# Attention weights times values: one product of 512 columns in fp32 becomes three passes of 256 columns, and moves in the order of a block

## The reference, cut to what matters

```
scores = einsum("bqhrd,bshrd->bhrqs", qi, k) * scale - slopes * dist
probs  = softmax(scores, axis=-1)
w      = probs[:, :, 0] - lam * probs[:, :, 1]
o      = einsum("bhqs,bshe->bqhe", w, v)        # the product that is changed
o      = rms_norm(o, subln_g) * (1 - lam_init)
y_attn = o * silu(g)
```

## Time and profile before

| | us |
|---|---|
| median of 3 runs (lowest to highest) | 3786.94 (3786.23 to 3787.26) |
| the profiled execution, its own time | 3784.53 |
| its span, first to last instruction | 3782.8 |
| PE busy / DVE busy / ACT busy, share of the span | 95% / 60% / 44% |
| attention stage, first transposes to last | 1652 to 2284 |
| mean granted clock of PE | 0.98 |

### The profile page before, as it was taken

The page is one execution under the profiler, slowest core; times in us unless marked ns, Lnnn a source line. Parts: engine busy times, 40 slices in busy tenths (PEclk is TensorE's granted clock), DMA queues, the critical chain, the costliest instruction groups (busy, mean ns, idle before and its releaser), DMA issues.

```text
span 3782.8 us, 48362 instructions
## 1 busy us (share of the span) xinstructions
PE 3609.8 (95%) x20222; PEld 3036.7 (80%) x20222; DVE 2251.6 (60%) x2947; ACT 1668.6 (44%) x2123; POOL 468.9 (12%) x373
## 2 busy tenths in 40 slices
PE   8999989999998999999999989999999999999998
PEld 7778968888876787877777759978777888778998
DVE  4545353456666765655656662468889888843332
ACT  4333344431114544467667772145455554442132
POOL 0001032200000121200000000012222222210001
PEclk9999999999999899999999999999999999999999
DMA  3012023342212011011111123121111111153111
GB/s 110 23 40 90 26 81 109 112 159 89 89 69 90 23 34 40 18 51 34 37 28 34 29 86 140 42 82 34 45 45 39 56 51 45 34 213 110 45 40 67
DMA packets 227389, 244.85 MB, mean 65 GB/s; under 512 B 10007, under 2 KB 190180, under 8 KB 227172
## 3 DMA queue, kind: packets, MB, share of 16 engines
q1 hardware_dynamic: 222391, 224.92, 18.4%
q10 hardware_dynamic: 4781, 16.84, 1.2%
HBM read 191.40 MB, written 50.33 MB: 64 GB/s over the span
## 4 chain that ended last, share of the span: by engine, by line
PE 77%; DVE 12%; ACT 5%; issue 3%; DMA 1%; POOL 0%; SPq 0%; ACTq 0%; DVEq 0%; POOLq 0%
PE pd L211 63%; PE pq L211 11%; PE pd L366 2%; DVE t L3520 2%; DVE t L328 1%; DVE t L3528 1%; PE pq L366 1%; DVE t L3965 1%; ACT t L3125 1%; ACT t L320 1%; DVE t L3952 0%; DVE t L3950 0%; DVE t L3197 0%; DVE t L2078 0%; DVE t L3215 0%
## 5 line engine op out<-in xcount | busy, mean ns | idle before, releaser
L211 PE MATMUL pd<-t 128*128 128x512 f32 (+2 forms) x15104 | 2904.1, 353 | 32.5 <-ACT t L3716 9.8
L211 PEld LDWEIGHTS pd<-t 128*128 128x128 f32 x15104 | 2407.6, 191 | 459.8 <-issue 90.9
L211 PE MATMUL pq<-t 128*128 128x128 f32 (+5 forms) x3782 | 635.7, 330 | 75.0 <-DVE t L4001 15.7
L211 PEld LDWEIGHTS pq<-t 128*128 128x128 f32 (+2 forms) x3782 | 484.3, 181 | 187.4 <-issue 44.4
L320 ACT ACTIVATE t<-t 128x2048 fp32r<-128x2048 f32 (+3 forms) x133 | 212.6, 1599 | 633.2 <-PE pd L211 590.8
L328 DVE TENSOR_TENSOR t<-t 128x2048 fp32r<-128x2048 f32 (+3 forms) x133 | 257.3, 1935 | 173.7 <-ACT t L320 173.2
L1919 DVE TENSOR_TENSOR t<-pd,t 128x512 f32<-128x512 f32 x256 | 172.9, 689 | 104.9 <-PE pd L211 102.7
L3248 DVE COPY t<-pd 128x512 f32<-128x512 f32 x64 | 44.2, 691 | 218.6 <-PE pd L366 218.6
L3528 DVE SCALAR_TENSOR_TENSOR t<-t 128x1024 f32<-128x1024 f32 x120 | 173.8, 1448 | 0.5
L3520 DVE SCALAR_TENSOR_TENSOR t<-t 128x1024 f32<-128x1024 f32 x120 | 169.1, 1409 | 2.1
L3917 POOL TENSOR_TENSOR t<-t 128x512 f32<-128x512 f32 x56 | 96.0, 1714 | 592.8 <-ACT t L3861 299.4
(11 more groups left out here) (345 smaller groups left out, 2830.8 us busy)
## 6 DMA issues: line engine op xcount, KB each, us to landing
t<-in_w_in_dram SPq DMA_DIRECT2D x97, 512.0 KB, 4.3
t<-in_w_out_dram SPq DMA_DIRECT2D x20, 1024.0 KB, 5.4
t<-in_w_in_dram SPq DMA_DIRECT2D x16, 1024.0 KB, 5.3
t<-in_w_mlp_dram SPq DMA_DIRECT2D x64, 256.0 KB, 3.5
u_scratch<-t SPq DMA_DIRECT2D x64, 256.0 KB, 3.3
t<-in_w_mlp_dram SPq DMA_DIRECT2D x16, 1024.0 KB, 5.0
t<-u_scratch SPq DMA_DIRECT2D x15, 1024.0 KB, 7.2
t<-in_x_dram SPq DMA_DIRECT2D x16, 512.0 KB, 9.2
```

Of the source, the lines that this page charges most:

```text
L211: ins = e.matmul(out, l, r, start=(first and j == 0), stop=(last and j == n - 1), skip_group_check=True)
```

## The change

The product AV is formed per two blocks (256 columns) and not per four, in split parts: 24 matmuls of 128x256 for each quarter of a head in place of 8 fp32 matmuls of 128x512 for each half. For that:

- `WT` becomes two tiles of [128, 8, 256], high and low part, so it holds two blocks. ACT copies both groups of transposes as high parts (`wTh`), and DVE then subtracts to get the low parts (`wTc`). Both groups' banks are freed by DVE's `wTc`.
- The values are split likewise: ACT's copy gives the high part (`avh`), DVE's new `dve_att_vt` the low part (`avt`), and this frees the bank of vt.
- PE's order in block n becomes: [tt in 6, 7: vt]; [tt in 2, 5: ms]; projection of the next head; [tt even, n > 0: AV of the two blocks before]; scores(n+2); wT(n,0), wT(n,1).
- ACT reads each quarter of AV right behind the exponentials of n+2 (square and copy of 256 columns), ahead of its copies of wT(n). The order of the other steps of ACT and DVE stays.
- The ring `tmp` has 6 tiles in place of 4, and two waits name the last quarter of AV.

```diff
@@ -2857,10 +2857,16 @@
     QS = [[w[:, 1024:2048] for w in WH], [sbt(ph, [128, S], F32R) for _ in range(2)]]
     KS = [[w[:, 1024:2048] for w in WL[0:2]], [sbt(ph, [128, S], F32R) for _ in range(2)]]
     KL = [[WL[2][:, 1024:2048], sbt(ph, [128, S], F32R)], [sbt(ph, [128, S], F32R) for _ in range(2)]]
-    AB = [[sbt(ph, [128, S]), sbt(ph, [128, NT, 128])] for _ in range(2)]
+    AB = []
+    for _ in range(2):
+        raw = ExitStack()
+        gT32 = sbt(raw, [128, S])
+        v32 = sbt(raw, [128, NT, 128])
+        raw.close()
+        AB.append([sbt(ph, [128, S]), sbt(ph, [128, NT, 128], F32R), sbt(ph, [128, NT, 128], F32R), v32])
     SR = ring(ph, 3, [128, 2, S])
-    WT = sbt(ph, [128, 8, 512])
-    tmp = ring(ph, 4, [128, 512])
+    WT = [sbt(ph, [128, 8, 256], F32R) for _ in range(2)]
+    tmp = ring(ph, 6, [128, 512])
     sm = ring(ph, 4, [128, 8])
     epsc = sbt(ph, [128, 1])
     ph.close()
@@ -2918,7 +2924,7 @@
                 pe_att_fm(e, 0, kind, th)
 
     def act_att_out(e, h, kind, th):
-        gT, vt_ = AB[h % 2]
+        gT = AB[h % 2][0]
         sl, b = half(th), PD.of("a" + kind, h, th)
         e.wait_ge(*at["a" + kind, h, th])
         if kind in "qk" and h >= 2:
@@ -2950,9 +2956,17 @@
     def act_att_vt(e, h, th):
         e.wait_ge(*at["avT", h, th])
         if h >= 2:
-            e.wait_ge(*at["AV", h - 2, 1])
+            e.wait_ge(*at["AV", h - 2, 3])
         e.copy(AB[h % 2][1][:, th * 4:th * 4 + 4, :], four(PD.of("avT", h, th)[:, :])).then_inc(
-            *at.inc("act", "avt", h, th, free=("avT", h, th)))
+            *at.inc("act", "avh", h, th))
+
+    def dve_att_vt(e, h, th):
+        sl = slice(th * 4, th * 4 + 4)
+        e.wait_ge(*at["avh", h, th])
+        if h >= 2:
+            e.wait_ge(*at["AV", h - 2, 3])
+        e.tensor_tensor(AB[h % 2][2][:, sl, :], four(PD.of("avT", h, th)[:, :]), AB[h % 2][1][:, sl, :].bitcast(F32),
+                        SUB).then_inc(*at.inc("dve", "avt", h, th, free=("avT", h, th)))
 
     def dve_att_out(e, h, kind, th):
         sl, b = half(th), PD.of("a" + kind, h, th)
@@ -3011,14 +3025,16 @@
 
     def pe_att_values(e, n, bank):
 
-        h, th = n // 8, n // 4 % 2
-        b = at_bank(e, bank, "AV", h, th)
-        for m in range(n, n + 4):
+        h, q = n // 8, n // 2 % 4
+        b = at_bank(e, bank, "AV", h, q)
+        for m in range(n, n + 2):
             for q2 in range(2):
                 e.wait_ge(*at["wTc", m, q2])
         e.wait_ge(*at["avt", h, 0])
         e.wait_ge(*at["avt", h, 1])
-        mms(e, b[:, :], [(AB[h % 2][1][:, j, :], WT[:, j, :]) for j in range(8)]).then_inc(*at.inc("pe", "AV", h, th))
+        _, vh, vl, _ = AB[h % 2]
+        mms(e, b[:, 0:256], [p for j in range(8) for p in three(vh[:, j, :], vl[:, j, :], WT[0][:, j, :],
+                                                                WT[1][:, j, :])]).then_inc(*at.inc("pe", "AV", h, q))
 
     def pe_stage_att(e):
         for th in range(2):
@@ -3036,10 +3052,6 @@
         turns = cycle((2, 3))
         for n in range(BLOCKS):
             h, tt = divmod(n, NT)
-            if n + 2 < BLOCKS:
-                pe_att_scores(e, n + 2)
-            if tt % 4 == 0 and n:
-                pe_att_values(e, n - 4, next(turns))
             if tt >= 6 and h < 7:
                 pe_att_vt(e, h + 1, tt - 6, next(turns))
             if owed(n)[0] >= 0:
@@ -3048,6 +3060,10 @@
                 if tt % 2 == 0:
                     pe_att_unit(e, h + 1, KIND[tt])
                 pe_att_fm(e, h + 1, KIND[tt], tt % 2, n % 2)
+            if tt % 2 == 0 and n:
+                pe_att_values(e, n - 2, next(turns))
+            if n + 2 < BLOCKS:
+                pe_att_scores(e, n + 2)
             if n in (62, 63):
                 pe_o2_first(e, n - 62)
             for q2 in range(2):
@@ -3056,7 +3072,7 @@
                 s = SR.of("s", n)
                 transposed(e, b, [s[:, 0, tile(q2 * 4 + j)] for j in range(4)]).then_inc(*at.inc("pe", "wT", n, q2))
             at.also("pe", ("s", n))
-        pe_att_values(e, 60, next(turns))
+        pe_att_values(e, 62, next(turns))
         pe_o2_first(e, 2)
         pe_att_ms(e, 7, 1, next(turns))
         ended("att", "pe")
@@ -3075,7 +3091,7 @@
             pe_done(o2_unit[-1])
 
     def back_in(k):
-        return [KL[0][1].bitcast(F32), flat(AB[0][1])][k % 2]
+        return [KL[0][1].bitcast(F32), flat(AB[0][3])][k % 2]
 
     def sp_o2_fetch(e, k):
         if k >= 2:
@@ -3083,7 +3099,7 @@
         elif k == 0:
             e.wait_ge(*at["scores", 6, 7, 1])
         else:
-            e.wait_ge(*at["AV", 6, 1])
+            e.wait_ge(*at["AV", 6, 3])
         e.dma(back_in(k)[:, :], YM[k * 128:(k + 1) * 128, :], "y2a", k)
 
     def act_o2_split(e, k):
@@ -3109,13 +3125,14 @@
             e.activation(q[:, :], q[:, :], ACT.Exp, scale=-0.5).then_inc(*at.inc("act", "ors", h, th))
 
     def act_att_values(e, n):
-        h, th = n // 8, n // 4 % 2
-        b = PD.of("AV", h, th)
-        o = e.take(tmp, "o", h, th)
-        q = e.take(tmp, "osq", h, th)
-        e.wait_ge(*at["AV", h, th])
-        e.activation(q[:, :], b[:, :], ACT.Square).then_inc(*at.inc("act", "osq", h, th))
-        e.copy(o[:, :], b[:, :]).then_inc(*at.inc("act", "o", h, th, free=("AV", h, th)))
+        h, q4_ = n // 8, n // 2 % 4
+        th, c = q4_ // 2, slice(q4_ % 2 * 256, q4_ % 2 * 256 + 256)
+        b = PD.of("AV", h, q4_)
+        o = tmp.of("o", h, th) if q4_ % 2 else e.take(tmp, "o", h, th)
+        q = tmp.of("osq", h, th) if q4_ % 2 else e.take(tmp, "osq", h, th)
+        e.wait_ge(*at["AV", h, q4_])
+        e.activation(q[:, c], b[:, 0:256], ACT.Square).then_inc(*at.inc("act", "osq", h, th))
+        e.copy(o[:, c], b[:, 0:256]).then_inc(*at.inc("act", "o", h, th, free=("AV", h, q4_)))
 
     def act_stage_att(e):
         def scores(n):
@@ -3161,16 +3178,17 @@
             act_att_ms(e, *owed(n))
             if n + 2 < BLOCKS:
                 scores(n + 2)
-            if tt % 4 == 0 and n:
-                act_att_values(e, n - 4)
-            e.wait_ge(*at["wT", n, 0])
-            e.copy(WT[:, 0:4, tile(tt % 4)], four(PD.of("wT", n, 0)[:, :])).then_inc(
-                *at.inc("act", "wTc", n, 0, free=("wT", n, 0)))
+            if tt % 2 == 0 and n:
+                act_att_values(e, n - 2)
+            for q2 in range(2):
+                e.wait_ge(*at["wT", n, q2])
+                e.copy(WT[0][:, q2 * 4:q2 * 4 + 4, tile(tt % 2)], four(PD.of("wT", n, q2)[:, :])).then_inc(
+                    *at.inc("act", "wTh", n, q2))
             for k in SPLIT_AT.get(n, []):
                 act_o2_split(e, k)
             if n == 61:
                 act_unit(e)
-        act_att_values(e, 60)
+        act_att_values(e, 62)
         act_att_ms(e, 7, 1)
 
     def dve_att_ms(e, h, th):
@@ -3218,7 +3236,9 @@
         scans_ended(e)
         dve_att_setup(e)
         dve_unit(e)
+        dve_att_vt(e, 0, 0)
         dve_att_out(e, 0, "k", 0)
+        dve_att_vt(e, 0, 1)
         dve_att_out(e, 0, "k", 1)
         dve_unit(e)
         for th in range(2):
@@ -3242,11 +3262,16 @@
                 dve_o2_split(e, k)
             if 0 < n < 57:
                 dve_att_out(e, (n - 1) // NT + 1, KIND[tt - 1], (tt - 1) % 2)
-            e.wait_ge(*at["wT", n, 1])
-            if tt % 4 == 0 and n:
-                e.wait_ge(*at["AV", h if tt else h - 1, 0 if tt else 1])
-            e.tensor_copy(WT[:, 4:8, tile(tt % 4)], four(PD.of("wT", n, 1)[:, :])).then_inc(
-                *at.inc("dve", "wTc", n, 1, free=("wT", n, 1)))
+            if tt >= 6 and h < 7:
+                dve_att_vt(e, h + 1, tt - 6)
+            if tt % 2 == 0 and n:
+                e.wait_ge(*at["AV", h if tt else h - 1, (tt // 2 + 3) % 4])
+            for q2 in range(2):
+                sl = slice(q2 * 4, q2 * 4 + 4)
+                e.wait_ge(*at["wTh", n, q2])
+                e.tensor_tensor(WT[1][:, sl, tile(tt % 2)], four(PD.of("wT", n, q2)[:, :]),
+                                WT[0][:, sl, tile(tt % 2)].bitcast(F32), SUB).then_inc(
+                    *at.inc("dve", "wTc", n, q2, free=("wT", n, q2)))
             if h < 7 and tt % 2 == 0:
                 dve_unit(e)
             if tt in (3, 6):
```

## The result

The changed kernel takes 4153.9 us (median of 4 runs, 4152.17 to 4158.81) against 3787.1 of the kernel before on the same chip: a ratio of 1.0969, interval 1.0953 to 1.0984. 367 us were added where 330 were forecast; the time lies inside the range. The profiled execution is the slowest of the four, 4158.8 us.

What follows compares the result with a forecast made beforehand. PE was taken to bound the kernel. To the profiled 3784.5 us it added 223 for seven heads (waits and changed PE work), 10 for the last head and 97 for the clock: 4114.5, as median 4117, range 4010 to 4175.

Steps and rivals of the forecast that it cites:

- (a): Even blocks: PE waits 4.7 us before wT(n,1) for AV's bank, freed by ACT's copy behind the exponentials of n+2.
- (e): Projection of tt 4 waits 2.7 us for the bank of tt 2's q, whose low part DVE takes behind reductions.
- (d): Bank of vt, freed by DVE's subtraction: at tt 6 a share of (a)'s 4.7 us, at tt 7 a 2.4 us wait.
- (b): ms at tt 2 and vt at tt 6 wait 4.9 us each for wT(n-1,0)'s bank, freed by DVE's subtraction.
- (c): ms at tt 5 and vt at tt 7, which follow even blocks, wait 0.8 us each.
- PE's work: Per head, PE's matmuls and transposes at full clock: projections, scores, transposes, AV quarters, ms and vt, 79.6 us.
- The clock: Slower PE clock after waits: 2.1 us for each of six long waits, 12.6 per head, +97 us in all.
- The last head: Attention's last head, which has no projections: waits add 10 us, between +5 and +16, and the clock 9 more.
- The clock did not stay up: Rival 1, whole kernel: same waits but no slowing of PE's clock, 4020 us; chance 0.16.
- The bank alone did not bind: Rival 2, attention stage: only AV's bank makes PE wait, (b) to (e) mostly hidden, 3973 us; chance 0.10.
- The projection did not hide the hand-overs: Rival 3, attention stage: the projection hides the bank hand-overs, leaving only the 17.6 us gain, 3769 us; chance 0.07.
- rival 4: AV's short matmuls: weight loads bound them at 0.15 us each, 23 us on top, 4140 us; chance 0.05.

Runs made afterwards that it cites:

- Run 10: The changed kernel with two of the three passes of AV left out, high times high only: 4100.0 us, 1.0824.
- run 5: The changed kernel with 15 useless matmuls ahead of wT(n,0) at tt 0, 2 and 4 of the first seven heads: 4160.6 us, 1.0976.
- run 4: The changed kernel with 34 useless matmuls ahead of wT(n,0) at tt 0, 2 and 4 of the first seven heads: 4113.7 us, 1.0858.
- run 3: The changed kernel with ACT's square and copy of AV moved ahead of the exponentials of n+2: 4092.4 us, 1.0807.
- run 1: The changed kernel with PE issuing scores(n+2) first in block n: 3863.1 us, 1.0205.
- run 2: The kernel before, in fp32 with no split, with only PE's order changed to that of the change: 4089.4 us, 1.0800.
- run 7: The changed kernel with PE's order of before (scores, AV, vt, ms, projection, transposes): 3882.4 us, 1.0247.
- run 8: The kernel before with AV per two blocks, still in fp32 and in its own order: 3814.2 us, 1.0067.
- run 6: The changed kernel with DVE's low parts of projection and values taken ahead of the reductions of n+2: 4112.6 us, 1.0847.

## Why the prediction was right

**The waits (a) to (e)** were right one by one. Forecast 35.3 us per head, measured 34.6. (a) and (d) share the wait at tt 6, so they are compared together: 18.8 + 2.4 = 21.2 forecast, 15.8 + 5.5 = 21.3 measured. (The wait at tt 6 comes in two pieces, 2.92 for DVE's low part ahead of `wT(n,0)` and 1.22 for ACT's copy ahead of `wT(n,1)`.) (b): 4.9 each, measured 5.2 and 5.0. (e): 2.7, measured 3.1. (c), forecast at 0.8 each, does not show in the list. The links behind them hold too: DVE started 1.71 us after the first matmul of the scores where 1.39 was taken; square and copy of 256 columns start 0.28 apart, the copy takes 0.37, against 0.27 and 0.38. These two were said to be by proportion, but half of 0.49 and 0.58 would be 0.25 and 0.29, so the recorded working does not give them.

**PE's work** of 79.6 per head cannot be read directly, since the clock stretches it to 98.2. Run 10 supports the price of AV: 54 us for 512 matmuls left out is 0.11 each. The period 133.1 leaves 18.9 for the clock beside 79.6 and 34.6.

**The clock** is the term that was mis-sized: 12.6 us per head forecast, about 18.6 measured (98.2 less 79.6). The step that failed is "I charge 2.1, the row nearest in length, to the six": it lets the two short waits go free. One head shows it; it has five waits near 5 us and three near 3, where six and two were forecast. The stretches below run from the end of a wait to the start of the next, PE busy all but 0.1 us of them except in the third, which holds the wait of 1.22, and follow waits of 4.82, 5.19, 2.92, 2.83 and 3.09 us:

```profile
2047.35:2057.71 10.36, 10.36 (x44) 8.46 (x44) 5.13 (x9) 4.37 (x7) 0.00 (x0) 0.85 0.15 35
2062.90:2076.89 13.99, 13.99 (x62) 11.02 (x62) 2.72 (x5) 8.21 (x10) 0.00 (x0) 0.83 0.00 0
2013.63:2026.81 13.18, 11.86 (x48) 9.24 (x48) 5.71 (x9) 5.46 (x11) 0.00 (x0) 0.77 0.14 38
2029.63:2042.53 12.90, 12.90 (x64) 10.87 (x64) 3.47 (x6) 8.50 (x12) 0.00 (x0) 0.87 0.00 1
2095.03:2107.52 12.49, 12.42 (x60) 10.40 (x60) 4.89 (x8) 5.07 (x8) 0.00 (x0) 0.87 0.23 63
```

At the prices of full clock that the prediction uses, the work in them is 8.62 (0.44 + 5.46 + 1.85 + 0.87, for transposes, projection, scores, transposes), 11.52, 9.06, 11.07 and 10.63 us. So PE lost 1.7 and 2.5 us behind the two long waits and 2.8, 1.8 and 1.8 behind the three short ones (the 2.8 may be due in part to the 1.22). Over the eight such stretches of the head the loss is 12.0 us behind the five long waits, 2.4 each, and 6.4 behind the three short ones, 2.1 each, in sum 18.4. The price of 2.1 was nearly right, and that the short waits go free was wrong; run 5 says the same. The upper bound, all eight at 2.1, is 16.8 and nearer. The Trainium skill (TensorE: Matmul & The Clock Gate, A second HAM failure mode: psum-queue depth-cycling) describes a kernel whose PE idles briefly between groups of matmuls as it cycles through PSUM banks, and whose clock swings between its two rates. This trace agrees: 0.85 of full clock in a stage whose PE waits for PSUM banks.

**The sum.** The profiled execution is 44 us above the 4114.5 of the sum. The seven intervals from Silu to Silu grew by 342 where 223 + 88 = 311 were forecast, the last head by 23 where 19 were forecast, and the parts outside by 9.

**The last head**: +10 and +9 for the clock forecast, +23 measured, at a clock of 0.80. PE idles 17.5 us more and saves 2.2 of work, so the waits give +15.3, near the upper end of the forecast's +5 to +16; the rest, about 7.5, is clock. In the recorded sum three pairs of 19.3, the first 3 less and ms 2 more, come to 57 and not 60.

**Rivals.** The clock did not stay up: it is at 0.85, and run 4 shows what that costs. The bank alone did not bind (run 3). The projection did not hide the hand-overs, because it lies ahead of the scores (runs 1 and 2). The passes did pay as matmuls: rival 4's 0.15 us each would have made run 10 77 us faster, and it was 54. What the split costs lies elsewhere. In the old order it is 96 us: 25 for the quarters and about 70 for what stands between transposes and AV, the copies and subtractions among it (runs 7 and 8). The prediction priced these only inside the waits of the changed order, where they count; it did not ask what they cost in any other order.

## What to carry to other kernels

In this pipeline of three engines the order within PE's stream mattered more than its work: what starts a round trip through other engines is to be issued ahead of the longest piece of independent work, not behind it. One moved call was worth 291 us here, the saving it accompanied 17.6 at best. Before a buffer's reader is changed, look at what stands ahead of it in that engine's stream, and price PE's waits twice: once as time, once as clock.

## What was not expected of the hardware

Useless matmuls in a wait made the kernel 40 us faster, at full dose; at less than half the dose they gave nothing. Short waits cost clock too: behind three waits of 2.8 to 3.1 us PE lost 2.1 us each, behind five of about 5 it lost 2.4 each. Nor does the period follow the work in proportion: runs 4, 6 and 10, with quite different work, all have a period of 126.3 us in three to five of the six intervals behind the first. Why the same value comes back is not settled. And a load of ACT's function table, 1.28 us, did not lengthen the wait at tt 0 (4.82 us, like its neighbours), though it stands right ahead of the exponentials: it ended at 2040.31, and ACT then idled 4.09 us until DVE had reduced the scores.
